# A two-way split float32r trunk kernel: six matmuls of 272 columns per weight block become five, of 364, 272, 364, 272 and 360 columns

## What is computed

```python
def mixer(xn, conv_prev, w_in, ln_g, ln_b, w_s, b_s, conv_w, w_pa, w_pb, w_o):
    z = xn @ w_in
    u_a, v_a, bg, cg, hh, ga, gb = jnp.split(z, SPLIT_IDX, axis=-1)
    u = jax.nn.gelu(u_a, approximate=False)
    v = layernorm(jax.nn.gelu(v_a, approximate=False), ln_g, ln_b)
    a = u * spatial_gate(v, w_s, b_s)
    xc = jnp.concatenate([conv_prev, cg * hh], axis=1)
    conv = conv_w[0] * xc[:, :L] + conv_w[1] * xc[:, 1:L + 1] + conv_w[2] * xc[:, 2:]
    bconv = bg * conv
    m = jax.nn.sigmoid(ga) * (a @ w_pa) + jax.nn.sigmoid(gb) * (bconv @ w_pb)
    return m @ w_o, xc[:, -(CONV_WIDTH - 1):], v

def trunk(...):
    x = x + mixer(rmsnorm(x, norm_mix), ...)
    g = rmsnorm(x, norm_ffn)
    x = x + (jax.nn.silu(g @ w_gate) * (g @ w_up)) @ w_down
    return rmsnorm(x, norm_final), new_conv, new_v
```

## Time and profile before

| | before |
|---|---|
| median of 3 runs | 944.7 us |
| the profiled execution's own time | 944.17 us |
| its span in the trace | 942.4 us |
| TensorE (PE) busy | 922.2 us, 98% |
| VectorE (DVE) busy | 512.6 us, 54% |
| ScalarE (ACT) busy | 259.4 us, 28% |
| GpSimd (POOL) busy | 62.9 us, 7% |
| DMA | 83.5 MB, 28% of 16 engines |
| TensorE clock granted | full from 20.7 us to the end of the matmuls |

### The profile page before, as it was taken

How to read it: one execution, slowest core, us unless ns; L and a number is a source line. 1 busy time by engine, 2 the same in 40 slices (tenths; PEclk the granted TensorE clock), 3 DMA queues, 4 the chain that set the end, 5 groups by cost and what they waited for, 6 DMA issues and landing times.

```text
span 942.4 us, 17750 instructions
## 1 busy us (share of the span) xinstructions
PE 922.2 (98%) x7273; PEld 917.0 (97%) x7273; DVE 512.6 (54%) x923; ACT 259.4 (28%) x378; POOL 62.9 (7%) x64
## 2 busy tenths in 40 slices
PE   6999999999998999999999999999999999999995
PEld 6999999999998999999999999999999999999995
DVE  4567777666566333355578655555533355555452
ACT  7333332223233333222211211222212122112331
POOL 0000010000004000000024200000000000000330
PEclk8999999999999999999999999999999999999998
DMA  9221232221222222222222222222223422221312
GB/s 282 94 73 63 90 96 90 86 73 64 89 89 70 72 85 88 90 89 89 89 90 90 90 90 90 89 89 67 67 84 116 134 82 80 78 65 48 90 48 95
DMA packets 90230, 83.50 MB, mean 89 GB/s; under 512 B 1612, under 2 KB 88756, under 8 KB 90196
## 3 DMA queue, kind: packets, MB, share of 16 engines
q1 hardware_dynamic: 90196, 83.03, 28.0%
HBM read 80.65 MB, written 2.38 MB: 88 GB/s over the span
## 4 chain that ended last, share of the span: by engine, by line
PE 97%; DMA 1%; issue 0%; SPq 0%; DVE 0%; ACT 0%; ACTq 0%; DVEq 0%
PE ps_main L425 32%; PE ps_main L423 31%; PE ps_main L424 31%; DMA tok<-in_x_prompt_dram 1%; PE ps_g L544 1%; PE ps_g L455 0%; PE ps_t L455 0%; PE ps_g L545 0%; PE ps_g L464 0%; PE ps_t L529 0%; PE ps_t L448 0%; SPq L325 0%; PE ps_main L630 0%; ACT tok L808 0%; ACTq L109 0%
## 5 line engine op out<-in xcount | busy, mean ns | idle before, releaser
L423 PE MATMUL ps_main<-act_hi,w_hi 128*128 128x272 f32 x2336 | 676.5, 290 | 3.2 <-DVE sig L861 3.2
L425 PE MATMUL ps_main<-act_hi,w_lo 128*128 128x272 f32 x2336 | 677.5, 290 | 0.0
L424 PE MATMUL ps_main<-act_lo,w_hi 128*128 128x272 f32 x2336 | 672.8, 288 | 0.0
L423 PEld LDWEIGHTS ps_main<-act_hi,w_hi 128*128 128x128 f32 x2336 | 440.8, 189 | 4.3 <-DVE sig L861 3.4
L424 PEld LDWEIGHTS ps_main<-act_lo,w_hi 128*128 128x128 f32 x2336 | 441.4, 189 | 0.2 <-issue 0.2
L425 PEld LDWEIGHTS ps_main<-act_hi,w_lo 128*128 128x128 f32 x2336 | 440.1, 188 | 0.0
L645 ACT CAST w_hi<-w_raw 128x2048 fp32r<-128x2048 f32 x50 | 95.3, 1906 | 283.6 <-PE ps_main L425 283.5
L848 DVE TENSOR_TENSOR w_lo<-w_raw,w_hi 128x2048 fp32r<-128x2048 f32 x50 | 128.0, 2559 | 48.2 <-ACT w_hi L645 48.0
L650 ACT ACTIVATE w_hi<-w_raw,g_cols 128x256 fp32r<-128x256 f32 x224 | 92.5, 496 | 97.8 <-PE ps_main L425 97.4
L854 DVE SCALAR_TENSOR_TENSOR w_lo<-w_raw,g_cols,w_hi 128x256 fp32r<-128x256 f32 x224 | 91.4, 480 | 47.6 <-ACT w_hi L650 47.3
L1153 DVE TENSOR_TENSOR gate_sb<-ps_main,r_all 128x544 f32<-128x544 f32 x22 | 16.0, 725 | 73.6 <-PE ps_main L425 73.3
(11 more groups left out here) (151 smaller groups left out, 364.2 us busy)
## 6 DMA issues: line engine op xcount, KB each, us to landing
w_raw<-in_w_in_dram SPq DMA_DIRECT2D x27, 1024.0 KB, 5.1
w_raw<-in_w_gate_dram SPq DMA_DIRECT2D x11, 1024.0 KB, 5.3
w_raw<-in_w_up_dram SPq DMA_DIRECT2D x11, 1024.0 KB, 5.3
w_raw<-in_w_down_dram SPq DMA_DIRECT2D x8, 768.0 KB, 4.7
w_raw<-in_w_down_dram SPq DMA_DIRECT2D x8, 640.0 KB, 4.3
w_raw<-in_w_pa_dram SPq DMA_DIRECT2D x4, 1024.0 KB, 4.9
w_raw<-in_w_pb_dram SPq DMA_DIRECT2D x4, 1024.0 KB, 5.0
w_raw<-in_w_o_dram SPq DMA_DIRECT2D x4, 1024.0 KB, 5.0
```

The source lines that it names most:

```text
L423: pe.matmul(out, whi, xhi, start=(k == 0), stop=False)
L424: pe.matmul(out, whi, xlo, start=False, stop=False)
L425: last = pe.matmul(out, wlo, xhi, start=False, stop=(k == blocks - 1))
```

## The change

The two activation tensors become one, `feat` [128, 24 blocks, 2 halves, 544], in which each half holds its 272 high columns followed by its 272 low columns. For each block the high weights multiply 364 neighbouring columns of a half (272 high and the first 92 low), for each half, and then the remaining 180 low columns of both halves in one matmul of 360 columns; the low weights multiply the 272 high columns of each half. `ps_main` takes three banks per pair, so that the partial sums of the low columns lie beside the others, and `ps_t` and `ps_g` become one tensor `ps_m` of two banks. What the low columns gave is copied out of PSUM by ScalarE (`take_low`, two copies per tile) and added by VectorE (`take_sum`), after which the elementwise operation that used to read PSUM reads SBUF. Both halves of a tile now end together.

```diff
-            def product_half(p, j, s, i, h, blocks, x0, width, ready=None):
...
-                    pe.matmul(out, whi, xhi, start=(k == 0), stop=False)
-                    pe.matmul(out, whi, xlo, start=False, stop=False)
-                    last = pe.matmul(out, wlo, xhi, start=False, stop=(k == blocks - 1))
-                last.then_inc(tile_half, 1)
+            def high_by_half(p, s, i, h, k, x0):
+                whi, _ = weights(p, s, i, k)
+                pe.matmul(ps_main[:, p.pair(s, i), h, 0:HALF + LA], whi, feat[:, x0 + k, h, 0:HALF + LA],
+                          start=(k == 0), stop=False)
+            def high_by_rest(p, s, i, k, x0, blocks):
+                whi, _ = weights(p, s, i, k)
+                return pe.matmul(ps_main[:, p.pair(s, i), 2, 0:2 * LC].rearrange("p (h n) -> p h n", h=2), whi,
+                          feat[:, x0 + k, :, HALF + LA:N], start=(k == 0), stop=(k == blocks - 1))
+            def low_by_half(p, s, i, h, k, x0, blocks):
+                _, wlo = weights(p, s, i, k)
+                pe.matmul(ps_main[:, p.pair(s, i), h, 0:HALF], wlo, feat[:, x0 + k, h, 0:HALF],
+                                 start=False, stop=(k == blocks - 1))
+            def product(p, s, i, blocks, x0, ready=None, behind={}):
+                for k in range(blocks):
+                    for h in range(2):
+                        if ready is not None:
+                            ready(k, h)
+                        high_by_half(p, s, i, h, k, x0)
+                        low_by_half(p, s, i, h, k, x0, blocks)
+                    last = high_by_rest(p, s, i, k, x0, blocks)
+                    if k == blocks - 1:
+                        last.then_inc(tile_half, 2)
+                    if (i, k) in behind:
+                        behind[i, k]()
...
+            def take_low(p, j, s, i, out):
+                pair = p.pair(s, i)
+                act.wait_ge(tile_half, 2 * p.tile(j, s, i) + 2)
+                x = halves(out)
+                act.copy(x[:, :, 0:LA], ps_main[:, pair, 0:2, HALF:HALF + LA])
+                act.copy(x[:, :, LA:HALF],
+                         ps_main[:, pair, 2, 0:2 * LC].rearrange("p (h n) -> p h n", h=2)).then_inc(low_ready, 1)
...
-            def take_times_r(p, j, s, i, out, r):
-                done(p, j, s, i)
-                dve.tensor_tensor(halves(out), ps_main[:, i, :, 0:HALF], halves(r[:]),
-                                  ALU.mult).then_inc(dve_out[i], 2)
+            def take_sum(p, j, s, i, out, low):
+                dve.wait_ge(low_ready, p.tile(j, s, i) + 1)
+                pair = p.pair(s, i)
+                dve.tensor_tensor(halves(out), ps_main[:, pair, 0:2, 0:HALF], halves(low),
+                                  ALU.add).then_inc(dve_out[pair], 1)
+                dve.wait_ge(dve_out[pair], p.out_before(j, s, i) + 1)
+            def take_times_r(p, j, s, i, out, r, low=None):
+                take_sum(p, j, s, i, out, out if low is None else low)
+                dve.tensor_tensor(out, out, r[:], ALU.mult).then_inc(dve_out[i], 1)
...
             def turn_v(t):
                 pe.wait_ge(gelu_done, t + 1)
+                if t:
+                    pe.wait_ge(v_in_tok, t)
+                else:
+                    pe.wait_ge(rx_ready, 1)
...
+            def turn_rows():
+                pe.wait_ge(v_in_tok, 1)
+            def turn_ws():
+                pe.wait_ge(v_in_tok, 2)
...
                 def mix_positions(i):
                     if i == 1:
                         pe.wait_ge(gate_out, g)
+                    elif isinstance(j, int):
+                        pe.wait_ge(bias_ready, KD)
```

More of the change, by code:

```diff
@@ L293, in fbits, with hi_of, lo_of, in_halves @@
             return ap.bitcast(F32)
+        def hi_of(block):
+            return feat[:, block, :, 0:HALF]
+        def lo_of(block):
+            return feat[:, block, :, HALF:N]
+        def in_halves(a, b):
+            return [(h, max(a, h * HALF), min(b, (h + 1) * HALF)) for h in range(2)
+                    if max(a, h * HALF) < min(b, (h + 1) * HALF)]
         block = ctx.enter_context(nc.Block())
@@ L372, in _ @@
                 load(ph["merge_a"], j, 1, w_pa, j)
+            with sp.Fori(0, 4) as j:
+                load(ph["merge_b"], j, 0, w_in, j + GB)
+                load(ph["merge_b"], j, 1, w_pb, j)
             sp.wait_ge(states_ready, 1)
@@ L438, in unit @@
                     pair_free(p, j, s, i)
-                    for h in range(2):
-                        product_half(p, j, s, i, h, blocks, x0, 2 * P if p.per_unit == 2 else P,
-                                     ready if i == 0 and s == 0 else None)
-                        if (i, h) in behind:
-                            behind[i, h]()
+                    product(p, s, i, blocks, x0, ready if i == 0 and s == 0 else None, behind)
             def turn_blocks(out, src, rows):
@@ L587, in norm_sums @@
                 for c in range(CH + 1):
-                    last = pe.matmul(ps_t[0:ROWS[c], 0, c:c + 1], sq_sum[:, c * P:c * P + ROWS[c]],
+                    last = pe.matmul(ps_m[0:ROWS[c], 1, sums_at + c:sums_at + c + 1], sq_sum[:, c * P:c * P + ROWS[c]],
                                      ones[:, 0:1], start=True, stop=True)
                 last.then_inc(sums_turned, 1)
-            unit(p, 0, 0, XN, ready=xg_there, behind={(0, 1): norm_sums, (1, 0): lambda: spread(r_diag, diag_ready, CH + 1, r_turned)})
+            unit(p, 0, 0, XN, ready=xg_there, behind={(0, KD - 1): norm_sums, (1, KD // 2 - 1): lambda: spread(r_diag, diag_ready, CH + 1, r_turned)})
             unit(p, 0, 1, XN)
@@ L735, in _, with take_lows @@
             p = ph["merge_a"]
-            act.wait_ge(states_turned, 1)
-            act.copy(states_out[:], ps_t[0:4 * KD, 0, 0:P]).then_inc(states_ready, 1)
+            act.wait_ge(gate_out, KD)
+            act.wait_ge(staged, KD)
+            def take_lows(p, j, s):
+                for i in range(2):
+                    take_low(p, j, s, i, acc[:, i, :])
             with act.Fori(0, 4) as j:
@@ L750, in _, with silus @@
                     split_hi(ph["out"], j, s)
-            def silus(p, j):
+                    take_lows(ph["out"], j, s)
+            def silus(p, j, norm=None):
                 for i in range(2):
+                    take_low(p, j, 0, i, acc[:, i, :])
+                    if norm is not None and i == 0:
+                        act.wait_ge(msq_done, norm)
+                        act.activation(root[:], msq[:], ACT.Sqrt).then_inc(root_done, 1)
                     act.wait_ge(dve_out[i], p.out_before(j, 0, i) + 2)
@@ L775, in _, with take_y_low @@
                 split_hi(p, j, 1)
+                take_lows(p, j, 1)
             p = ph["down_2"]
+            def take_y_low(j, s, first=False):
+                if not first:
+                    act.wait_ge(y_turned, 2 * j + s - 1)
+                    act.wait_ge(ysq_done, 2 * j + s - 1)
+                take_low(p, j, s, 0, x_last[:, s, :])
             def y_squares(j, s, first=False):
@@ L791, in _ @@
             split_hi(p, 0, 0)
+            take_y_low(0, 0, first=True)
             split_hi(p, 0, 1)
             y_squares(0, 0, first=True)
+            take_y_low(0, 1, first=True)
             split_hi(p, 1, 0)
```

350 lines of the change are left out of this document (181 added, 169 removed).

## The result

The changed kernel takes **959.5 us** (median of 4 runs, 959.04 to 962.53) against 944.5 of the kernel before: ratio 1.016, 95% interval 1.013 to 1.019. The forecast was 950: the direction was right, and the 5 us foretold are a third of the 15 that came. One run of the kernel with another split, further down, took 1290.6 us at a mean granted clock of 0.65, and is left out there. In the later groups of runs the kernel before took 945.6 to 946.4 us in place of 944.5; each ratio is to the kernel before of its own group, and differences of plain times across groups carry 1 to 2 us of that. The profiled execution took 959.25 us, its span 957.5, which is 15.1 above the 942.4 of before.

What follows compares the result with a forecast made beforehand. TensorE, busy 98% of the span, was taken to bound the kernel. From 944.2 us, -14.1 for matmuls, +15.9 for waits and the end, +3.4 for the clock gave 949.4, say 950; its own range 944 to 957.

Steps and rivals of the forecast that it cites:

- Rival A: Matmuls: the columns carry the extra, 0.461 ns each, so only some 3 us are saved; 960.5 us, chance 0.24.
- Rival B: Matmuls: the weight load sets the pitch, 704.2 ns a pair, 56.4 us saved; 907 us, chance 0.14.
- the three readings: Against weight loads setting the pitch: 0.113 us load spacing; full pitch with weights long loaded; 0.29 us matmul without load beside it.
- The six places: Places where TensorE has no cover for the rearranged, longer draining; together 15.9 us added.
- GELU: Phase v: `turn_v(0)` waits for GELU of tile 0, which follows two VectorE passes instead of one; +0.7 us.
- mixing weights: Phase v, tile 3: the mixing weights' transpose waits for VectorE's copy to `tok`, ending at 45.6 us; +3.0 us.
- layer norm: Layer norm chain from the copy of v through the c drain grows from 13.8 to 16.4 us; +1.5 us.
- bias: First position mixing now waits for the bias, while TensorE is there after one tile, 6.0 us; +6.4 us.
- merge: Old 3.2 us wait beside GpSimd's 9.6 us operation starts 1.6 us later, pair freed after two passes; +2.5 us.
- the end's drain: The last tile is drained as a whole, 0.75 + 0.73 + 0.73 in place of 0.44 us; +1.8 us.
- Rival C: The waits are half of those counted, because the queues catch up; 940 us, 936 to 946, chance 0.11.
- the cover: A whole tile (6.0 us) of TensorE work hides the longer draining; failing by 0.2 us per unit would cost 10 us.

Runs made afterwards that it cites:

- order: Changed kernel with each block's five matmuls grouped as 364, 364, 360, 272, 272 instead of alternating: 964.2 us, ratio 1.019 to the kernel before.
- residual: Changed kernel with GpSimd's sum of high and low x in eight one-block pieces instead of one operation: 951.8 us, ratio 1.006.
- splits: Changed kernel plus trailing blocks of five matmuls with eleven numbers of joined low columns, behind two leads: 740.2 ns a block with 112, 749.0 with 92.
- mixing weights: Changed kernel with the transposes of the mixing weights in the middle of v tile 4 instead of tile 3: 959.9 us.
- the first experiment: Changed kernel plus a trailing row of matmuls of 64 to 512 columns: start-to-start pitch 119.9 ns at 256 columns, 226.7 at 512.

## Why the prediction missed

**The matmuls failed.** "12.1 ns x 1168 = -14.1 us" came out as -5.9. The step that failed is the sentence that took 12.1 ns per instruction "because one figure for every matmul of one shape is all that the rows show". The owner of the extra was right for widths from 256 up, as the experiment shows, but its size was carried from 272 columns to 364 and 360: foretold 163.8, 162 and 125.4 ns, measured in the feed-forward 166.5, 166.4 and 124.7. A block so took 8.5 ns more than foretold, 9.9 us, and `merge_b` and `out` 0.8 us on top. Against that the kernel before took 755.0 ns a block where I read 752.5 off a window's count, 2.9 us the other way. These make 7.8 of the 8.2 us missing. Had the split been 112, the forecast's 740.5 ns would have been met (740.0), in part by luck, since that saves 15.0 ns from the true 755.0 and not 12.1. So the error lay in treating a shape's extra as exact to a nanosecond when the sum multiplied it by 5840. The lower bound of 3 us held, but the range took 8 to 16 for the saving without a ground for the 8, and 5.9 lies outside. Its own terms also add up to 959.1 at the top (944.2 - 8 + 15.9 + 7), not to the 957 given.

**Rival A came out near the total (960.5) for a wrong reason**: the columns do not carry the extra. Rival B is refuted: a block takes 749.0 ns and not 704, and 512 columns carry the extra beside a loader that is idle for a sixth of the time. Two of the three readings that I had against it were weak, since they rest on how long a matmul lasts, and the profile models the ends of matmuls; only starts count. The busy weight loader (96% after, 97% before) did not tell what a sixth fewer loads would bring. The Trainium skill's "Perfetto Trace Analysis", section "Identifying the Most-Contended Engine", has its busy share, beside the share of peak FLOP/s, as the measure of headroom: here each load lasts 188 ns and the next begins 120 to 175 ns after it, so that the share is near 100% in both kernels. The other page of the Trainium skill, "TensorE: Matmul & The Clock Gate", section "Back-to-back issue gap", has 2.5 ns beyond the columns; every width from 256 up shows 12 to 16 here.

**The six places were right**, the largest within 0.3 us: GELU 0.8 (0.7 foretold), mixing weights 2.2 (3.0), layer norm 1.8 (1.5), bias 6.1 (6.4), merge 4.9 (5.7), the end's drain 1.9 (1.8): from the last product matmul's start to the small matmuls of the last sums it is 1.6 us before and 3.5 after. Together, with the merge's wait counted as 1.7 more than before (2.5 foretold), 14.5 against 15.9. The mixing weights' list ended at 45.0 us, foretold 45.6; VectorE in phase v (columns as above):

```profile
39.56 3.26 DVE L957 SCALAR_TENSOR_TENSOR w_lo<-w_raw,g_cols,w_hi 128x256 fp32r<-128x256 f32 x8 [4.65 <-ACT w_hi L711]
42.74 0.72 DVE L965 TENSOR_TENSOR gelu_v<-ps_main,gelu_v 128x544 f32<-128x544 f32 x1
43.49 0.72 DVE L972 TENSOR_TENSOR gelu_v<-gelu_v,r_x 128x544 f32<-128x544 f32 x1
44.13 0.68 DVE L1020 COPY tok<-ps_m 128x512 f32<-128x512 f32 x1
44.73 0.27 DVE L1022 COPY tok<-ps_m 32x128 f32<-32x128 f32 x1
```

Rival C (half the waits) falls, and the cover that I kept in the range only, for every unit, held.

**The clock was undersized**: 3.4 foretold, 4.2 behind the bias and the merge (1.85 and 2.35), and 1.6 more at the end, which I had not counted: in the kernel before it stayed up until 935.5 us, behind the small matmuls of the last sums, and in the changed one it fell at 944.5, in their midst. Where it fell later the end was shorter: 15.3 us in place of 16.8 in the run with the residual in pieces, where it fell 5.8 us behind the last product matmul in place of 3.8. TensorE, timeline, one pair before and one behind the fall:

```profile
944.26 0.35 PE L682 MATMUL ps_main<-ones,y_sum 128*128 128x1 f32 x2
944.47 0.55 PE L683 MATMUL ps_main<-ones,y_sq 128*128 128x1 f32 x2
944.89 0.56 PE L682 MATMUL ps_main<-ones,y_sum 128*128 128x1 f32 x2
```

The start was 0.7 us later, and that is the clock too: it fell at 13.90 us before and at 12.65 after, so the eight transposes ahead of the first product ran at half from their first one on. Timeline, before and after:

```profile
13.22 1.36 PE L448 MATMUL ps_t<-ident,tok 128*128 128x128 f32 x8 [2.98 <-DMA tok<-in_x_prompt_dram]
13.30 1.97 PE L480 MATMUL ps_m<-ident,tok 128*128 128x128 f32 x8 [3.36 <-DMA tok<-in_x_prompt_dram]
```

It also rose 1.25 us sooner, so that phase v had part of this back. The steps together: 949.4 + 8.2 (matmuls) - 1.4 (waits) + 2.4 (clock) + 0.7 (start) = 959.3 us, the profiled 959.25. The matmuls' 8.2 is what the other steps leave, so that the sum closes by its making; 7.8 of it are found in the starts.

## What to carry to other kernels

A cost per instruction read from one shape is good to a few nanoseconds only, and is to be read from start to start, not from a window's count; before a split is chosen for a stream of thousands of matmuls, time several splits, as one constant here was worth 10 us. When a drain gets longer, list each place where a consumer is one step behind and follow the queue by hand: that part of the forecast held. And price a wait with the half clock behind it, then look for an engine's gap to put the late work in.

## What the hardware showed unexpectedly

- The extra of a float32r matmul is 13.2 to 13.4 ns at 256, 320, 400 and 512 columns and between 11.7 and 15.9 at the others from 272 to 448; at 64 columns it is 85. The same sequence can repeat in one of two patterns (749.0 or 753.4 ns with 92 joined, 740.0 or 760.0 with 80); with 92 joined one of them was kept for more than 300 us at a time. What chooses the pattern was not found; nothing in the traces names it.
- The half clock came behind waits of 6.1 and 4.9 us, but in four runs (order, residual, splits, mixing weights) also for 3.4 us behind one of about 2 us, where the changed kernel kept the full clock; and in the first experiment it came at 965.0 us where TensorE had not waited, behind 4.3 us of matmuls of 64 columns.
- VectorE's subtraction was 4.5 times as long beside one large GpSimd operation and ended 2.15 us behind it, while pieces of one block (1.36 us each) beside shorter VectorE work cost TensorE nothing.
